# Weights rounded ahead of the mixed value in the late projection, and a new order of steps in the RWKV core

## The chip, the cores and the metric

The kernel runs on one core of a Trainium2 chip. The metric is the device time of one execution in microseconds; three executions of the kernel before gave 2173.88 us as median (2173.66 to 2179.12). TensorE is PE (its weight loads PEld), VectorE DVE, ScalarE ACT, GpSimd POOL, SyncE SP.

## The reference, cut to what matters

Two layers work on 256 tokens of width 2048 in fp32. What the change touches is the end of the first layer's second branch and, in the second layer, the recurrence of RWKV-7 together with the output projection of the attention half:

```
# first layer
yb = einsum('blc,cd->bld', yb * silu(zb), w_out_b)        # "outb"
m  = sigmoid(ga) * ya + sigmoid(gb) * yb                  # the mixed value
x  = x + einsum('bld,de->ble', m, w_o)                    # "wo"
# second layer, per head of 64, one token after the other
sa    = state @ a
state = state * w + sa (x) bb + v (x) k
y     = state @ r
# and then
mixed = concatenate([attn, rwkv]); h = h + mixed @ w_out  # attn half: "wouta", rwkv half: "woutb"
```

## The kernel before

Weights stream from HBM in units of 128 x 1024 fp32 through a ring of four slots. Each unit is made into two fp32r parts: ACT rounds it (`w_hi`, L506 in `split_hi`), DVE takes the rest (`w_lo`, L996 in `split_lo`), and SP reloads the slot as soon as `lo_ready` counts the unit. PE multiplies three times for each 128 x 128 block: high by high, high by low, low by high (L1714 to L1716). A unit of eight blocks is 24 matmuls with 256 columns. `split_hi` of unit n waits until unit n-4 has been used, `split_lo` until `split_hi` is done, and PE until `lo_ready`.

**Late projection (`outb`, 16 column blocks of one unit each).** For block b, ACT first rounds the weights of unit b+3, then waits for `f_ready` and rounds the mixed value f (L696, `ms`). DVE makes the low part of unit b+3, waits until PE has used unit b, computes f from the PSUM bank in two steps (L1250, L1252) and then the low part of the mixed value of block b-1 (L1243). `wo` follows; its first column reads the 16 mixed blocks one by one and waits for each.

**RWKV core.** The recurrence is done in four chunks of 64 tokens; each needs the inverse of a 64 x 64 triangular matrix per head, which a chain of products on PE gives. All 16 heads work at once: two heads share the 128 rows (row halves 0 and 1), and a step is 16 or 32 small matmuls, with an evacuation by DVE or ACT between steps. PE's order within chunk i is n2 and n2t (in one step), vt, n4 and n4t, w2, first half of x, w4 and n8, second half of x, bkt (transposes), w8, qt and q, q2 and md, g0, g1, g2, mt, n, sa, y, s. The sums w2, w4, w8 are added to `m_w` by DVE (L1538, `plus`). g0 and g2 (L1988, `with_a_and_r`) multiply the b and k of the next chunk by its a and r, the first for row half 0, the second for row half 1; DVE masks their results (L1442, L1443, `masked_products`; gm0 and gm1) into `g_a` and `g_r`. n (`a_with_b`) overwrites the PSUM banks of g0, and sa those of g2, so they wait for gm0 and gm1. Dependences are counted in `core_mm`, `core_dve` and `core_act`, by the tables MM, DV and AC.

Between these steps PE fills in blocks of `wouta` (`wout(count)`, L2040 to L2042, three matmuls each; 16 units of eight blocks). After step s of a chunk it does what is left of that chunk's share, PART = (4, 4, 3, 2, 3) units. The first block of unit j waits until DVE has added the result of unit j-2 to the residual (`wout_add`, L1519 and L1521, semaphore `wa_free`). DVE also splits the weights of these units (`wout_lo`) and weights the bonus (`gate_bonus`, L1480) within its own order. A stage ahead of chunk 0 (L1988 on `ps_main`) prepares that chunk's matrices.

Of the kernel before, what the change touches and what calls it, by code (L numbers as in the profile page):

```python
# [15 lines left out]
P = 128  # L16
# [110 lines left out]
def hybrid_kernel(nc, wmain, wdown, bst_dram, cst_dram, par_dram, const_dram, x_dram, lora_dram,  # L127
                  gup_dram, bias_dram, out_dram):
    ctx = ExitStack()
    with ctx:  # L130
# [195 lines left out]
        def bu_at(t):  # L326
# [4 lines left out]
        PIECES = ((0, 2), (2, 4), (4, 8), (8, 12), (12, 16))  # L331

        MM = {n: k + 1 for k, n in enumerate(
            ["n2", "n2t", "vt", "n4", "n4t", "w2", "w4", "n8", "x", "bkt", "w8", "qt", "q", "q2", "md", "g0", "g1",
             "g2", "mt", "n", "sa", "y", "s"])}
        DV = {n: k + 1 for k, n in enumerate(
            ["n2", "n4", "w2", "w4", "w8", "qt", "t1", "q2", "gm0", "g1", "gm1", "sa", "nf", "w1", "s"])}
        AC = {n: k + 1 for k, n in enumerate(["n2t", "vt", "n4t", "n8", "x", "bkt", "q", "md", "mt", "sa", "y"])}

        MM_NEXT, DV_NEXT = ("g0", "g2", "n", "s"), ("gm0", "gm1", "nf", "w1", "s")  # L340
# [159 lines left out]
        def _(act):  # L500
# [184 lines left out]
            for b in range(8):  # L685
                split_hi(At(n0 + b + 3))
                act.wait_ge(unit_used, n0 + b + 1)
                if b >= 2:
                    act.wait_ge(yo_ready, b - 1)
                nc.scalar.activation(gt[:, b % 2, :], main[:, (g0 + b) % 4, 0:L], ACT.Sigmoid,  # L690
                                     bias=par_c("b_glu", b)).then_inc(bank_free[(g0 + b) % 4], 1)
            n0 = UNIT0["outb"]
            for b in range(16):
                split_hi(At(n0 + b + 3))
                act.wait_ge(f_ready, b + 1)
                nc.scalar.activation(mh[:, b, :], f[:, b % 2, :], ACT.Copy).then_inc(mh_ready, 1)  # L696
            n0 = UNIT0["wo"]
            with act.Fori(0, 4) as i:
                for b in range(4):
# [286 lines left out]
        def _(dve):  # L986
# [12 lines left out]
            def bank(g):  # L999
                return main[:, g.c % 4, 0:L]  # L1000

            def evac(ins, g):

                return ins.then_inc(bank_free[g.c % 4], 1)
# [241 lines left out]
            for b in range(16):  # L1246
                split_lo(At(n0 + b + 3))
                dve.wait_ge(unit_used, n0 + b + 1)
                g = At(g0 + b)
                evac(V.tensor_tensor(tmp[:, 0, :], bank(g), sgb[:, b, :], ALU.mult), g)  # L1250
                dve.wait_ge(bank_free[g.c % 4], g.turns(4, 1))
                V.tensor_tensor(f[:, b % 2, :], tmp[:, 0, :], sga[:, b, :], ALU.add).then_inc(f_ready, 1)  # L1252
                if b:
                    mixed_lo(b - 1)
# [190 lines left out]
            def diagonal_t(h):  # L1445
                return V.tensor_tensor(mat["nt"][hrow(h), :, :], ga[hrow(h), h, :, :], mask("mdiagt", h), ALU.mult)
# [66 lines left out]
            def wout_lo():  # L1513
                split_lo(At(n0 + taken[0] + 3))
                taken[0] += 1
# [8 lines left out]
            def chunk(i, last=False):  # L1524
# [3 lines left out]
                def done(name, ins):  # L1528
                    ins.then_inc(core_dve, steps(DV, DV_NEXT, name, last))
                    dve.wait_ge(core_dve, i * len(DV) + DV[name])  # L1530

                def take(name, dst):
                    mm(name)
                    done(name, V.tensor_copy(flat(dst), heads(OUT[name])))

                def plus(name, dst, old):
                    mm(name)
                    done(name, V.tensor_tensor(flat(dst), flat(old), heads(OUT[name]), ALU.add))  # L1538

                take("n2", mat["n2"])  # L1540
                if i:
                    wout_add()
                    centre(i - 1, main[:, first_column(i) % 2, :])
                    take("n4", mat["n4"])
                else:
                    gate_bonus(0)
                    take("n4", mat["n4"])
                wout_lo()
                plus("w2", mat["w"], mat["w"])
                plus("w4", mat["w"], mat["w"])  # L1550
                if not last:
                    mm("bkt")
                    stage(i + 1)
# [5 lines left out]
                    gate_bonus(1)  # L1559
                take("q2", mat["n4"])  # L1560
                wout_lo()
                if not last:
                    mm("g0")
                    done("gm0", masked_products(0, G0, grs[(i + 1) % 2]))
                plus("g1", mat["n4t"], mat["n2t"])
                if not last:
                    diagonal_t(0)
                    mm("g2")
                    done("gm1", masked_products(1, G2, grs[(i + 1) % 2]))
                    diagonal_t(1)  # L1570
                    mm("n")
                    diagonal(OUT["n"])
                mm("sa")
                done("sa", V.tensor_copy(st[hrow(0), :, 0, :], by_head(OUT["sa"])[hrow(0), :, :]))
                if not last:
                    done("nf", rest(OUT["n"]))
                    done("w1", V.tensor_tensor(mat["w"][:, :, :], mat["nt"][:, :, :], eye, ALU.add))
                    if i:
                        gated(i - 1)
                        group_out(i - 1)  # L1580
                    mm("s")
                    link(V.tensor_tensor(state[:, :, :], state[:, :, :],
                                         S.rearrange("p (j n) -> p j n", n=CH), ALU.add))
                    done("s", V.tensor_tensor(state[:, :, :], state[:, :, :], pc[:, :, i:i + 1].to_broadcast([P, 8, CH]),
                                              ALU.mult))
                    for _ in range(PART[i] - 2):
                        wout_add()
                        wout_lo()
                else:
                    gated(i - 1)  # L1590
                    group_out(i - 1)
                    rwkv_low(1, slice(0, 2 * CH))
                    rwkv_low(2, tokens(2))
# [106 lines left out]
        def _(pe):  # L1700
# [281 lines left out]
                        ins = nc.tensor.matmul(head(banks, j, h), *fn(j, h), start=False, stop=(j % 4 == 3))  # L1982
                return ins

            def with_a_and_r(i, h, banks):

                for j in range(8):
                    ins = nc.tensor.matmul(banks[:, j // 4, (j % 4) * P:(j % 4 + 1) * P],  # L1988
                                           bkc[hrow(h), j, :, :].rearrange("p a n -> p (a n)"),
                                           abr[hrow(h), :, j, toks(i)], start=True, stop=True)  # L1990
                return ins

            def a_with_b(i, banks):
# [23 lines left out]
            pair_probs(PAIRS - 1)  # L2017
            pe.wait_ge(staged, 1)
            pe.wait_ge(gate_sb, 2)
            with_a_and_r(0, 0, main[:, 0:2, :]).then_inc(core_pre, 1)  # L2020
            with_a_and_r(0, 1, main[:, 2:4, :]).then_inc(core_pre, 1)
            pair_output(PAIRS - 1)
            a_with_b(0, A).then_inc(core_pre, 1)
            pe.wait_ge(gr_taken, 1)
# [22 lines left out]
            for i in range(NCH):  # L2047
# [81 lines left out]
                ac("q")  # L2129
                two(("q2", "nt", "n"), ("md", "w", None))  # L2130
                ac("bkt")
                if not last:
                    pe.wait_ge(staged, i + 2)
                    done("g0", with_a_and_r(i + 1, 0, G0))
                else:
                    wout(3)
                dv("t1")
                dv("q2")
                ac("md")
                prod("g1", "n4", "n2t")  # L2140
                if not last:
                    done("g2", with_a_and_r(i + 1, 1, G2))
                else:
                    wout(2)
                dv("g1")
                prod("mt", "md", "n4t")
                if not last:
                    dv("gm0")
                    done("n", a_with_b(i + 1, OUT["n"]))
                    dv("gm1")  # L2150
                else:
                    wout(2)
                ac("mt")
                done("sa", every_head(OUT["sa"], lambda j, h: (mat["n2"][hrow(h), j, :], xv[hrow(h), j, :])))
                wout(3 if not last else 1)
                dv("sa")
                ac("sa")
                by_halves(OUT["y"], lambda j, h: (state[hrow(h), j, :], br[hrow(h), j, toks(i)]))
# [227 lines left out]
```

## Time and profile before

| | us |
|---|---|
| median of three runs | 2173.88 |
| the profiled execution | 2174.53 |
| its span | 2172.9 |
| mean granted clock of TensorE | 0.998 |

The spans of all rows are of this one profiled execution; 1.6 us of its time lie outside its span. By engine, the busy shares of the span are PE 98%, PEld 96%, DVE 71%, ACT 48%, POOL 12%. A matmul's end is modelled and matmuls overlap, so a short stop of PE shows best as the distance between two starts. `outb` runs from 769 to 817 us, the stage ahead of chunk 0 from 1231.8 us, and the four chunks start at 1242.1, 1281.5, 1318.8 and 1353.8 us.

### The profile page before, as it was taken

The numbers are of one execution on the slowest core, as the hardware profiler recorded it, in microseconds if no ns is written. First come the engines' busy times: TensorE is split into PE (matmuls) and PEld (weight loads), VectorE is DVE, ScalarE is ACT, GpSimd is POOL, SyncE is SP. The second block draws the span as 40 slices with busy tenths as digits, with TensorE's granted clock in tenths as the row PEclk, the third lists the DMA queues.
The fourth block names the chain that finished last, engine by engine and source line by source line (L and its number), as shares of the span: only waits on it lengthen the run. The fifth ranks groups of instructions, "written<-read, shape, count | busy, mean of one in ns | idle before, by whom it ended". The sixth has DMA issues, their size and how long they took to land.

```text
span 2172.9 us, 51647 instructions
## 1 busy us (share of the span) xinstructions
PE 2127.8 (98%) x20608; PEld 2075.7 (96%) x20608; DVE 1543.2 (71%) x2015; ACT 1033.6 (48%) x1342; POOL 267.0 (12%) x178
## 2 busy tenths in 40 slices
PE   7999999999999999999999999999999999999997
PEld 7999999999999999999999889899999999999997
DVE  7889999999745677768867767776666666654554
ACT  6544444444454445556444454654444444444443
POOL 0354444445200000000001000000000000000000
PEclk9999999999999999999999999999999999999999
DMA  7555555555656556655655311355555655556654
GB/s 265 184 169 182 178 184 190 182 182 181 202 192 192 190 201 203 197 176 166 210 181 189 105 61 52 108 176 193 193 192 193 193 194 192 194 180 199 192 190 138
DMA packets 107106, 387.84 MB, mean 178 GB/s; under 512 B 12032, under 2 KB 12160, under 8 KB 106752
## 3 DMA queue, kind: packets, MB, share of 16 engines
q1 hardware_dynamic: 104400, 375.44, 52.9%
q0 software_dynamic: 2176, 9.78, 1.3%
q8 instruction: 74, 1.21, 0.2%
q10 hardware_dynamic: 432, 1.21, 0.1%
q14 instruction: 24, 0.20, 0.0%
HBM read 384.29 MB, written 2.10 MB: 178 GB/s over the span
## 4 chain that ended last, share of the span: by engine, by line
PE 79%; DVE 14%; issue 4%; ACT 2%; DMA 0%; DVEq 0%; SPq 0%; ACTq 0%
PE ps_main L1714 24%; PE ps_main L1715 23%; PE ps_main L1716 23%; DVE w_lo L996 6%; ACT w_hi L506 1%; DVE m L1155 1%; DVE m L1156 1%; PE ps_aux L2069 1%; DVE acc L1162 1%; PE ps_main L2040 1%; PE ps_main L2041 1%; PE ps_main L2042 1%; PE ps_main L1956 1%; DVE g_scan L1165 0%; DMA w_raw<-wmain 0%
## 5 line engine op out<-in xcount | busy, mean ns | idle before, releaser
L996 DVE TENSOR_TENSOR w_lo<-w_raw,w_hi 128x1024 fp32r<-128x1024 f32 x718 | 916.6, 1293 | 419.5 <-ACT w_hi L506 411.7
L506 ACT ACTIVATE w_hi<-w_raw 128x1024 fp32r<-128x1024 f32 x718 | 748.4, 1048 | 711.7 <-PE ps_main L1716 656.6
L1714 PE MATMUL ps_main<-xs,w_hi 128*128 128x256 f32 x1664 | 463.2, 278 | 7.6 <-DVE w_lo L996 6.6
L1715 PE MATMUL ps_main<-xs,w_hi 128*128 128x256 f32 x1664 | 460.2, 277 | 0.0
L1716 PE MATMUL ps_main<-xs,w_lo 128*128 128x256 f32 x1664 | 460.2, 277 | 0.0
L1714 PE MATMUL ps_main<-x3s,w_hi 128*128 128x256 f32 x1408 | 389.3, 276 | 0.0
L1715 PE MATMUL ps_main<-x3s,w_hi 128*128 128x256 f32 x1408 | 388.8, 276 | 0.0
L1716 PE MATMUL ps_main<-x3s,w_lo 128*128 128x256 f32 x1408 | 388.8, 276 | 0.0
L1714 PEld LDWEIGHTS ps_main<-xs,w_hi 128*128 128x128 f32 x1664 | 312.9, 188 | 16.0 <-DVE w_lo L996 11.6
L1716 PEld LDWEIGHTS ps_main<-xs,w_lo 128*128 128x128 f32 x1664 | 312.4, 188 | 0.0
L1715 PEld LDWEIGHTS ps_main<-xs,w_hi 128*128 128x128 f32 x1664 | 312.4, 188 | 0.0
L1714 PEld LDWEIGHTS ps_main<-x3s,w_hi 128*128 128x128 f32 x1408 | 264.3, 188 | 1.0 <-issue 1.0
L1715 PEld LDWEIGHTS ps_main<-x3s,w_hi 128*128 128x128 f32 x1408 | 264.3, 188 | 0.0
L1716 PEld LDWEIGHTS ps_main<-x3s,w_lo 128*128 128x128 f32 x1408 | 264.3, 188 | 0.0
L1714 PE MATMUL ps_main<-ns,w_hi 128*128 128x256 f32 x816 | 229.2, 281 | 0.1
L1716 PE MATMUL ps_main<-ns,w_lo 128*128 128x256 f32 x816 | 226.3, 277 | 0.0
L1715 PE MATMUL ps_main<-ns,w_hi 128*128 128x256 f32 x816 | 226.2, 277 | 0.0
L1714 PE MATMUL ps_main<-act,w_hi 128*128 128x256 f32 x704 | 194.3, 276 | 0.0
L1715 PE MATMUL ps_main<-act,w_hi 128*128 128x256 f32 x704 | 194.3, 276 | 0.0
L1716 PE MATMUL ps_main<-act,w_lo 128*128 128x256 f32 x704 | 194.3, 276 | 0.0
L1714 PEld LDWEIGHTS ps_main<-ns,w_hi 128*128 128x128 f32 x816 | 153.9, 189 | 7.4 <-issue 7.2
L1715 PEld LDWEIGHTS ps_main<-ns,w_hi 128*128 128x128 f32 x816 | 153.2, 188 | 0.2 <-issue 0.2
(428 smaller groups left out, 3724.4 us busy)
## 6 DMA issues: line engine op xcount, KB each, us to landing
w_raw<-wmain SPq DMA_DIRECT2D x622, 512.0 KB, 3.6
w_raw<-wdown SPq DMA_DIRECT2D x80, 512.0 KB, 3.7
w_raw<-wdown SPq DMA_DIRECT2D x16, 256.0 KB, 2.7
bias<-bias POOLq DMA_DIRECT2D x8, 384.0 KB, 3.4
x_res<-xt POOLq DMA_DIRECT2D x4, 512.0 KB, 7.0
out<-x_res SPq DMA_DIRECT2D x3, 512.0 KB, 2.8
x_first<-xt SPq DMA_DIRECT2D x2, 512.0 KB, 6.9
x_first<-xt ACTq DMA_DIRECT2D x2, 512.0 KB, 9.5
```

What stands on the lines that cost most here:

```text
L506: nc.scalar.activation(whi[:, s, 0:width], raw[:, s, 0:width], ACT.Copy).then_inc(hi_ready, 1)
L996: V.tensor_tensor(wlo[:, s, 0:width], raw[:, s, 0:width], whi[:, s, 0:width].bitcast(F32), ALU.subtract)\
L1155: V.tensor_tensor(m1[:, :, :], bu, cb, ALU.mult)
L1156: V.tensor_tensor(m2[:, :, :], bu, sb_, ALU.mult).then_inc(bu_used, 1)
L1162: link(V.tensor_tensor(g[:, 1, :], m1[:, 1, :], m2[:, 0, :], ALU.subtract))
L1714: nc.tensor.matmul(out, whi[:, s, w], high[:, k, :], start=(first and kk == 0), stop=False)
L1715: nc.tensor.matmul(out, whi[:, s, w], low[:, k, :], start=False, stop=False)
L1716: ins = nc.tensor.matmul(out, wlo[:, s, w], high[:, k, :], start=False, stop=(last and kk == kbs - 1))
L1956: ins = nc.tensor.matmul(head(banks, j, h), *fn(j, h), start=True, stop=True)
L2040: nc.tensor.matmul(out, whi[:, s, w], atth[:, k, :], start=(k == 0), stop=False)
L2041: nc.tensor.matmul(out, whi[:, s, w], attl[:, k, :], start=False, stop=False)
L2042: ins = nc.tensor.matmul(out, wlo[:, s, w], atth[:, k, :], start=False, stop=(k == 7))
```

## The change

Three things are changed.

First, in `outb`, ACT rounds the mixed value of block b-1 after the weights of unit b+3, not that of block b; DVE gets a wait on `f_ready` of the block before, ahead of writing `tmp` again.

Second, in the core's order on DVE: w2's sum comes right behind n4's copy, ahead of the weights' low part; in chunk 0 that low part and `gate_bonus(0)` move behind w4's sum. g1's sum moves ahead of gm0, and the two `diagonal_t` behind nf.

Third, in the core's order on PE: g0 and g2 become one step of 16 matmuls that alternates between the row halves, behind g1; four blocks of `wouta` take g0's old place, two more stand behind mt, and two in place of three behind sa.

```diff
+            def mixed_hi(j):
+                act.wait_ge(f_ready, j + 1)
+                nc.scalar.activation(mh[:, j, :], f[:, j % 2, :], ACT.Copy).then_inc(mh_ready, 1)
+
             for b in range(16):
                 split_hi(At(n0 + b + 3))
-                act.wait_ge(f_ready, b + 1)
-                nc.scalar.activation(mh[:, b, :], f[:, b % 2, :], ACT.Copy).then_inc(mh_ready, 1)
+                if b:
+                    mixed_hi(b - 1)
+            mixed_hi(15)
...
@@ DVE, outb
                 g = At(g0 + b)
+                if b:
+                    dve.wait_ge(f_ready, b)
                 evac(V.tensor_tensor(tmp[:, 0, :], bank(g), sgb[:, b, :], ALU.mult), g)
...
@@ DVE, chunk(i)
                 if i:
                     wout_add()
                     centre(i - 1, main[:, first_column(i) % 2, :])
-                    take("n4", mat["n4"])
-                else:
+                take("n4", mat["n4"])
+                plus("w2", mat["w"], mat["w"])
+                if i:
+                    wout_lo()
+                plus("w4", mat["w"], mat["w"])
+                if not i:
+                    wout_lo()
                     gate_bonus(0)
-                    take("n4", mat["n4"])
-                wout_lo()
-                plus("w2", mat["w"], mat["w"])
-                plus("w4", mat["w"], mat["w"])
...
                 wout_lo()
+                plus("g1", mat["n4t"], mat["n2t"])
                 if not last:
                     mm("g0")
                     done("gm0", masked_products(0, G0, grs[(i + 1) % 2]))
-                plus("g1", mat["n4t"], mat["n2t"])
-                if not last:
-                    diagonal_t(0)
                     mm("g2")
                     done("gm1", masked_products(1, G2, grs[(i + 1) % 2]))
-                    diagonal_t(1)
                     mm("n")
                     diagonal(OUT["n"])
...
                     done("nf", rest(OUT["n"]))
+                    diagonal_t(0)
+                    link(diagonal_t(1))
                     done("w1", V.tensor_tensor(mat["w"][:, :, :], mat["nt"][:, :, :], eye, ALU.add))
...
@@ PE
-            def with_a_and_r(i, h, banks):
-
+            def with_a_and_r(i, *banks):
+
+                ins = [None, None]
                 for j in range(8):
-                    ins = nc.tensor.matmul(banks[:, j // 4, (j % 4) * P:(j % 4 + 1) * P],
-                                           bkc[hrow(h), j, :, :].rearrange("p a n -> p (a n)"),
-                                           abr[hrow(h), :, j, toks(i)], start=True, stop=True)
+                    for h in range(2):
+                        ins[h] = nc.tensor.matmul(banks[h][:, j // 4, (j % 4) * P:(j % 4 + 1) * P],
+                                                  bkc[hrow(h), j, :, :].rearrange("p a n -> p (a n)"),
+                                                  abr[hrow(h), :, j, toks(i)], start=True, stop=True)
                 return ins
...
                 ac("bkt")
-                if not last:
-                    pe.wait_ge(staged, i + 2)
-                    done("g0", with_a_and_r(i + 1, 0, G0))
-                else:
-                    wout(3)
+                wout(4 if not last else 3)
                 dv("t1")
                 dv("q2")
                 ac("md")
                 prod("g1", "n4", "n2t")
                 if not last:
-                    done("g2", with_a_and_r(i + 1, 1, G2))
+                    pe.wait_ge(staged, i + 2)
+                    lower, upper = with_a_and_r(i + 1, G0, G2)
+                    done("g0", lower)
+                    done("g2", upper)
                 else:
                     wout(2)
                 dv("g1")
                 prod("mt", "md", "n4t")
                 if not last:
+                    wout(2)
                     dv("gm0")
...
-                wout(3 if not last else 1)
+                wout(2 if not last else 1)
```

**Order on ACT where `outb` begins.** `gt` is the last result of the projection before it, `ms` a mixed block. Before:

```order
L506 ACTIVATE w_hi<-w_raw 128x1024
L690 ACTIVATE gt<-ps_main,par 128x256
L506 ACTIVATE w_hi<-w_raw 128x1024
L696 ACTIVATE ms<-f_val 128x256
L506 ACTIVATE w_hi<-w_raw 128x1024
L696 ACTIVATE ms<-f_val 128x256
```

Now:

```order
L506 ACTIVATE w_hi<-w_raw 128x1024
L690 ACTIVATE gt<-ps_main,par 128x256
L506 ACTIVATE w_hi<-w_raw 128x1024 x2
L696 ACTIVATE ms<-f_val 128x256
L506 ACTIVATE w_hi<-w_raw 128x1024
L696 ACTIVATE ms<-f_val 128x256
```

The rows alternate as before, but each `ms` now belongs to the block before, so a weight unit no longer stands behind a mixed value that PE has yet to finish.

**Order on DVE where chunk 0 begins.** `m_n_139` and `m_n_141` are n2 and n4, `m_w` the sums, `sig_w` is `gate_bonus`, `bk_chunk` the staging of the next chunk. Before:

```order
L1534 COPY m_n_139<-ps_aux 128x512
L1480 SCALAR_TENSOR_TENSOR sig_w<-sig_w,par,out_gate_a 128x256 x4
L1534 COPY m_n_141<-ps_aux 128x512
L996 TENSOR_TENSOR w_lo<-w_raw,w_hi 128x1024
L1538 TENSOR_TENSOR m_w<-m_w,ps_aux 128x512 x2
L1366 COPY bk_chunk<-b_hat 64x8x64
```

Now:

```order
L1542 COPY m_n_139<-ps_aux 128x512
L1542 COPY m_n_141<-ps_aux 128x512
L1546 TENSOR_TENSOR m_w<-m_w,ps_aux 128x512 x2
L1002 TENSOR_TENSOR w_lo<-w_raw,w_hi 128x1024
L1488 SCALAR_TENSOR_TENSOR sig_w<-sig_w,par,out_gate_a 128x256 x4
L1374 COPY bk_chunk<-b_hat 64x8x64
```

The low part of the weights and the bonus have moved behind both sums, and stand ahead of the staging copies and of w8's sum.

**Order on PE in chunk 1, from the step behind q2 and md.** `ar_hat,bk_chunk` is the step with b and k, `m_n2t` g1, `m_n4t` mt, `bk_chunk,ar_hat` n, `x_chunk` sa, `att_h` a block of `wouta` (three rows each). Before:

```order
L2069 MATMUL ps_main<-const,m_w 64x64 x2
L1988 MATMUL ps_aux<-ar_hat,bk_chunk 128x128 x8
L1956 MATMUL ps_main<-m_n2t,m_n_141 64x64 x16
L1988 MATMUL ps_aux<-ar_hat,bk_chunk 128x128 x8
L1956 MATMUL ps_main<-m_n4t,m_md 64x64 x16
L1956 MATMUL ps_aux<-bk_chunk,ar_hat 64x64 x16
L1956 MATMUL ps_aux<-x_chunk,m_n_139 64x64 x16
```

Now:

```order
L2053 MATMUL ps_main<-att_h,w_lo 128x256
L1964 MATMUL ps_main<-m_n2t,m_n_141 64x64 x16
L1998 MATMUL ps_aux<-ar_hat,bk_chunk 128x128 x16
L1964 MATMUL ps_main<-m_n4t,m_md 64x64 x16
L2051 MATMUL ps_main<-att_h,w_hi 128x256
...
L1964 MATMUL ps_aux<-bk_chunk,ar_hat 64x64 x16
L1964 MATMUL ps_aux<-x_chunk,m_n_139 64x64 x16
```

The two steps of eight have become one of sixteen behind g1, with four blocks of the projection ahead of g1 and two between mt and n.

## Rows read from the trace of the kernel before

**Rows 1.** The page, busy time, share and instructions of each engine.

```profile
PE 2127.8 (98%) x20608; PEld 2075.7 (96%) x20608; DVE 1543.2 (71%) x2015; ACT 1033.6 (48%) x1342; POOL 267.0 (12%) x178
```

**Rows 2.** Waits of PE: waiting line, releaser, us in total, times, longest.

```profile
PE ps_aux L2069 <- DVE m_w L1538: 3.4, 3, 2.2
PE ps_main L1714 <- DVE ms L1243: 2.2, 1, 2.2
```

**Rows 3.** Timeline of ACT (start, us, line, tiles, idle before): end of glu, `outb`.

```profile
766.53 0.47 ACT L690 ACTIVATE gt<-ps_main,par 128x256 f32<-128x256 f32 x1 [1.30 <-PE ps_main L1716]
769.25 0.47 ACT L690 ACTIVATE gt<-ps_main,par 128x256 f32<-128x256 f32 x1 [1.30 <-PE ps_main L1716]
...
807.50 0.42 ACT L696 ACTIVATE ms<-f_val 128x256 fp32r<-128x256 f32 x1 [2.09 <-DVE f_val L1252]
807.83 1.04 ACT L506 ACTIVATE w_hi<-w_raw 128x1024 fp32r<-128x1024 f32 x1
810.96 0.42 ACT L696 ACTIVATE ms<-f_val 128x256 fp32r<-128x256 f32 x1 [2.09 <-DVE f_val L1252]
```

**Rows 4.** Timeline of DVE, one block of `outb`.

```profile
808.90 1.23 DVE L996 TENSOR_TENSOR w_lo<-w_raw,w_hi 128x1024 fp32r<-128x1024 f32 x1 [1.10 <-ACT w_hi L506]
810.04 0.42 DVE L1250 TENSOR_TENSOR tmp<-ps_main,sig_gb 128x256 f32<-128x256 f32 x1
810.50 0.43 DVE L1252 TENSOR_TENSOR f_val<-tmp,gate_a 128x256 f32<-128x256 f32 x1
```

**Rows 5.** Timeline of PE, first matmul of `outb`, and of `wo`'s k = 15.

```profile
769.04 0.28 PE L1714 MATMUL ps_main<-yos,w_hi 128*128 128x256 f32 x1
...
825.13 0.38 PE L1714 MATMUL ps_main<-ms,w_hi 128*128 128x256 f32 x1 [2.20 <-DVE ms L1243]
```

**Rows 6.** Timeline of PE, w4 and x of chunk 0, then of chunk 1.

```profile
1250.28 0.27 PE L2069 MATMUL ps_aux<-m_w,m_n 64*64 64x64 f32 x2 [2.17 <-DVE m_w L1538]
...
1251.49 1.92 PE L1975 MATMUL ps_aux<-stack,g_a 64*64 64x64 f32 x32
...
1288.48 0.27 PE L2069 MATMUL ps_aux<-m_w,m_n 64*64 64x64 f32 x2 [0.61 <-DVE m_w L1538]
...
1289.48 1.10 PE L1975 MATMUL ps_aux<-stack,g_a 64*64 64x64 f32 x32
```

**Rows 7.** Timeline of DVE, the two steps ahead of w2's sum in chunk 0.

```profile
1244.02 1.68 DVE L1480 SCALAR_TENSOR_TENSOR sig_w<-sig_w,par,out_gate_a 128x256 f32<-128x256 f32 x4
...
1248.32 1.23 DVE L996 TENSOR_TENSOR w_lo<-w_raw,w_hi 128x1024 fp32r<-128x1024 f32 x1 [1.75 <-ACT w_hi L506]
```

**Rows 8.** One stretch: busy time of each engine (instructions), granted clock, DMA share, GB/s.

```profile
1251.00:1254.40 3.40, 3.40 (x68) 3.28 (x60) 0.69 (x1) 1.78 (x3) 0.00 (x0) 0.50 0.35 130
```

**Rows 9.** Timeline of PE, the step with b and k: ahead of chunk 0, in chunk 1.

```profile
1231.80 3.47 PE L1988 MATMUL ps_main<-ar_hat,bk_chunk 64*128 64x128 f32 x32 [0.46 <-ACT out_gate_a L824]
...
1298.88 2.05 PE L1988 MATMUL ps_aux<-ar_hat,bk_chunk 64*128 64x128 f32 x16
1300.86 1.15 PE L1956 MATMUL ps_main<-m_n2t,m_n 64*64 64x64 f32 x32
1301.93 2.05 PE L1988 MATMUL ps_aux<-ar_hat,bk_chunk 64*128 64x128 f32 x16
```

**Rows 10.** Timeline of PE, a pair of row halves in the decay projection.

```profile
938.48 0.48 PE L1859 MATMUL ps_aux<-lora_lo,lora_up 64*128 64x256 f32 x1
938.48 0.48 PE L1860 MATMUL ps_aux<-lora_lo,lora_up 64*128 64x256 f32 x1
```

**Rows 11.** Timeline of PE and DVE: chunk 0's first sum; chunk 1, step s and behind.

```profile
1240.71 0.69 DVE L1474 TENSOR_TENSOR m_w<-m_nt,const 128x512 f32<-128x512 f32 x1
...
1310.41 1.10 PE L2164 MATMUL ps_aux<-stack,bk_tokens 128*64 128x64 f32 x32
1311.44 0.38 PE L2040 MATMUL ps_main<-att_h,w_hi 128*128 128x256 f32 x1
...
1313.54 0.42 DVE L1521 TENSOR_TENSOR x_res<-x_res,ps_main 128x256 f32<-128x256 f32 x1
```

More of the change, by code:

```diff
@@ L333, in hybrid_kernel @@
         MM = {n: k + 1 for k, n in enumerate(
-            ["n2", "n2t", "vt", "n4", "n4t", "w2", "w4", "n8", "x", "bkt", "w8", "qt", "q", "q2", "md", "g0", "g1",
+            ["n2", "n2t", "vt", "n4", "n4t", "w2", "w4", "n8", "x", "bkt", "w8", "qt", "q", "q2", "md", "g1", "g0",
              "g2", "mt", "n", "sa", "y", "s"])}
         DV = {n: k + 1 for k, n in enumerate(
-            ["n2", "n4", "w2", "w4", "w8", "qt", "t1", "q2", "gm0", "g1", "gm1", "sa", "nf", "w1", "s"])}
+            ["n2", "n4", "w2", "w4", "w8", "qt", "t1", "q2", "g1", "gm0", "gm1", "sa", "nf", "w1", "s"])}
         AC = {n: k + 1 for k, n in enumerate(["n2t", "vt", "n4t", "n8", "x", "bkt", "q", "md", "mt", "sa", "y"])}
@@ L2019, in _ @@
             pe.wait_ge(gate_sb, 2)
-            with_a_and_r(0, 0, main[:, 0:2, :]).then_inc(core_pre, 1)
-            with_a_and_r(0, 1, main[:, 2:4, :]).then_inc(core_pre, 1)
+            lower, upper = with_a_and_r(0, main[:, 0:2, :], main[:, 2:4, :])
+            lower.then_inc(core_pre, 1)
+            upper.then_inc(core_pre, 1)
             pair_output(PAIRS - 1)
```

## The prediction, made before the changed kernel had run

> **What bounds the kernel now.** I read the shares by engine first: PE is busy for 2127.8 us of a span of 2172.9 [rows 1], and DVE and ACT have room. So time can only come from work that PE no longer does, or from moments in which PE stands still. Then I read the waits of PE for whom it stands still: 3.4 us in three waits for `m_w`, and 2.2 us in one wait for `ms`, the low part of a mixed value [rows 2]. Both lie where the change is. The modelled ends hide part of such a stop, so I measure the stops by distances between starts.
>
> In `outb` the timeline of ACT shows the bound. In the projection before, one result follows the other after 2.72 us (766.53 to 769.25) [rows 3]: that is what PE needs for a unit of 24 matmuls, and ACT waits for PE. In `outb` it is 3.46 us (807.50 to 810.96), and ACT waits 2.09 us of each block for DVE's f [rows 3]. The cycle closes over two engines: `ms` starts at 807.50, the weights' high part at 807.83 for 1.04 us [rows 3], the low part at 808.90, tmp at 810.04, f at 810.50 for 0.43 us [rows 4], then the next `ms` at 810.96. PE is no member of it. The ring hides this for some blocks, then PE falls behind.
>
> **Part 1, the late projection.** PE begins `outb` at 769.04 and begins `wo`'s k-block 15 at 825.13, after the wait for `ms` [rows 5]. Between the two lie 16 units and 15 blocks of an eighth of a unit: 17.9 units. At 2.72 us they take 48.6 us, so a PE that never waits is there at 817.6. The difference is 7.5 us.
>
> Is PE unhindered after the change? ACT now rounds unit b+3 as soon as PE has used unit b-1, without waiting for f(b). High and low part take 1.04 + 1.23 = 2.3 us [rows 3, 4], and PE has three units (8.2 us) in hand. DVE does per block the low part (1.14, start to start), tmp and f (0.46 each) [rows 4] and the mixed low part (about as long as f, 0.4): 2.5 us in 2.72. ACT does 1.04 + 0.42. Both fit, DVE narrowly. The last mixed value: PE ends unit 15 at 769.04 + 43.5 = 812.6; tmp, f, high and low part come to 1.9 us, so 814.5, and PE asks for it at 817.6. The added wait on `f_ready` is for DVE's own previous step, and behind it stand only tmp and f; it costs nothing, since it is done one block earlier. **Term: -7.5 us**, between -7.0 (if DVE's narrow margin is missed by 0.03 us in each of 16 blocks) and -7.9.
>
> **Part 2, w2's sum.** In chunk 0, w4 starts at 1250.28 after 2.17 us of idle, for `m_w` [rows 6]. DVE has the bonus (1.68 us) and the weights' low part ahead of that sum, and the latter waits until 1248.32 for its high part [rows 7]. In chunk 1 the wait is 0.61 [rows 6]; all three together are 3.4 [rows 2], chunk 2's is about 0.2 since PE arrives late there. With the sum first, it is ready 0.9 us after w2 (0.04 to start, 0.69, 0.15 to PE), and the first half of x, 1.2 us, covers that. So all goes: -3.6. In chunk 0 the low part and the bonus (1.2 + 1.7) and the staging (1.5) now stand ahead of w8's sum, which comes 0.6 us too late for qt: +0.6. **Term: -3.0 us**, between -2.4 and -3.8.
>
> **Part 3, the clock.** Right behind the 2.17 us stop the granted clock is 0.50, the lower level of 1.2 GHz, for the 3.4 us from 1251.0, in which PE works throughout [rows 8]. The 16 products of x take 1.92 us there and 1.10 in chunk 1 [rows 6]. 3.4 us at half speed lose 1.7. The stop goes, so I count **-1.7 us**, between 0 and -1.7. The new stops below are 1.5 us or less; I give a fall 1 in 4.
>
> **Part 4, b and k in one step.** 16 matmuls ahead of chunk 0 take 3.47 us, 217 ns each, one after the other; in a chunk each eight take 1.98 us (1298.88 to 1300.86, and 1301.93 to the next step) [rows 9]. They use 64 rows each. Does the other half run beside it? The decay projection says so: two matmuls on opposite row halves, each with all 128 columns, start at the same 938.48 [rows 10]. So I take 16 in the time of eight, 1.98 us, three times: **-5.9 us**. Bounds: nothing gained (0) if the alternating loads of different weights keep them apart, since [rows 10] show only one pair at a time; the full -5.9 on the other side. I take the full value, because the rows are the same shape but for 128 columns of data in place of 256.
>
> Ahead of chunk 0 PE would gain another 1.7 us, but DVE is next: its masks start when the first half's result is there, which stays as it was, and its chain ends with the sum at 1240.71 + 0.69 [rows 11], less 0.15 us of idle between its masks. PE could start at 1241.3, and started chunk 0 at 1242.1: **-0.8 us**.
>
> **Part 5, the projection's blocks as filler.** Their number is fixed; only their places change. There are two stretches more in each of three chunks. The first matmul of a stretch is modelled at 0.38 us against 0.28 of one within [rows 5, 11], and leaving costs as much: 0.2 us a stretch, 6 stretches, **+1.2 us**, between 0.6 and 2. The Trainium skill has a rule here, in "TensorEngine Tiling (Array Packing)", section Key Properties: a change of the tiling mode drains the engine. If each of these 12 changes laid open what a matmul outlasts its successor's start by (0.28 less 0.11, so 0.17 us), this would be +2.0, and the sum 0.8 us later. By this rule the sum moves within its range.
>
> **Part 6, what is late next.** DVE. Taking chunk 1 in times of before, with g0's old start at 1298.88: four blocks (1.6 us), then g1 at 1300.5, b and k at 1301.6 to 1303.6, mt, two blocks (0.9), n at 1305.4, sa at 1306.4 (behind gm1, which DVE ends at 1306.2 after 2.6 us of masks), two blocks, y at 1308.4, s at 1310.6 to 1311.6. Sixteen blocks are left there, two units, and the second begins at 1314.4. It needs the add of the unit two before. On DVE stand ahead of it: masks until 1306.2, n's diagonal, sa's copy until 1308.2, nf 0.7, both diagonals 1.4, w1 0.7, the gate and output of the chunk before 2.3, the state 1.5, the add 1.0: 1315.8, where before it ended at 1313.96 [rows 11] and PE had 21 blocks left. PE waits 1.5 us. The same in chunk 0, without the gate and output but with 0.7 us less filler ahead: 0.6 us. g1 in chunk 0 waits 0.4 longer for q2's copy, which stands behind `gate_bonus(1)`; y waits 0.1 in each chunk; chunk 3 starts with a DVE that is 0.3 late for n4. **Term: +3.0 us**, between 1 and 5.
>
> **The sum.** -7.5 -3.0 -1.7 -5.9 -0.8 +1.2 +3.0 = -14.7 us. The profiled execution took 2174.5 (2172.9 of span and 1.6 around it), which gives 2159.8. The median of the runs is 0.65 us below it, so 2159.2 us. Behind the core nothing changes: chunk 3 and the 24 blocks behind it have the same order and end in the same wait.
>
> **The rivals.**
> - *The pair doesn't overlap.* 16 matmuls take 3.5 to 4.0 us. Part 4 gives nothing, and gm0 comes later. For it: each of the 16 has weights of its own; in [rows 9] PE goes at 217 ns per matmul with no overlap at all. Against it: [rows 10]. Price: 5.9 lost in the chunks and 1.1 ahead of chunk 0, where the first half's result comes 1.7 late: 2166.2 us. Chance 0.10.
> - *The half clock stays.* PE now has more short stops in chunk 0 (0.8, 0.5, 0.6, 0.7 us) and one of 1.5 behind chunk 1. Each fall as before costs 1.7. One remains: 2160.9; two: 2162.6. Chance 0.20.
> - *DVE is later still in the chunks' ends.* The adds wait for units, the units for adds: if every chunk's end cost 2 us rather than 1.5, 0.6 and 0, this would be +3.9: 2163.1. Chance 0.08.
> - *Slower than before.* The place is the core, 1231 to 1391 us; the mechanism the clock again, not as one dip but as a state: half-speed PE in front of late sums. With 30 us at 1.2 GHz the 14.7 us are gone, and beyond this it is slower; 45 us would give 2181.7. Against it: in the trace 3.4 us is all that the worst stop caused, and the stretches of projection are dense. Chance 0.02.
>
> **How the numbers follow.** Forecast 2159.2, chance 0.60 together with the small deviations of its terms. The rivals take 0.40. The low end, all terms at their good ends (-7.9, -3.8, -5.9, -0.8, -1.7, +0.6, +1), would be -18.5; I go two thirds of the way from -14.7, to 2156. The high end takes in one or two dips of the clock and the late DVE, and stops short of the pair that doesn't overlap: 2165. Outside lie 0.10 to 0.15 above and a little below. What a measurement of this kernel can tell from no change is about 0.3%, 6.5 us. The forecast, the clock's dips, the late DVE and even the pair that doesn't overlap (2166.2, 0.35% below) are faster; within 0.3% falls that last rival with a dip on top, and an `outb` that wins only half: 0.04. Slower: 0.02.
>
> **What would show it.** In `outb`, `ms` after `ms` at 2.72 us from the first block on, no wait of PE for `ms`, and `wo` reached 7.5 us earlier; a distance of over 2.8 would say that DVE is the bound. In the chunks, 16 matmuls of b and k within 2 us; no wait of w4 for `m_w`; no stretch at clock 0.50 behind 1240 us; new waits of the projection's first matmul (unit 3, unit 7) for `x_res` of L1521's successor, 0.6 and 1.5 us. The core's first step to `woutb` would shrink by 7.2 us. I am wrong if that sum is under 3 or if the distance in `outb` stays above 3 us.

## The result and the profile after

| | before | changed | ratio (95% interval) |
|---|---|---|---|
| first comparison, median us | 2174.31 | 2157.44 | 0.9913 (0.9897 to 0.9930) |
| profiled execution, us | 2174.53 | 2159.07 | |
| its span, us | 2172.9 | 2157.4 | |

The changed kernel is faster: by its ratio 18.9 us of the 2173.88 shown, by the two profiles 15.5. The forecast was -14.7, and 2159.2 us between 2156 and 2165; the ratio makes 2155.0. The shares by engine, against [rows 1]: PE's busy time is 9.8 us less (the paired steps and the half clock that is gone), the rest of the 15.5 is idle time.

```profile
PE 2118.0 (98%) x20608; PEld 2067.1 (96%) x20608; DVE 1544.4 (72%) x2015; ACT 1033.1 (48%) x1342; POOL 268.6 (12%) x178
```

I cut both traces at PE's first matmul of each stage and of each chunk; a distance between two such starts holds every stop and slow matmul in it.

| distance between starts, us | before | changed | difference | forecast |
|---|---|---|---|---|
| `outb` to `lora` (outb and wo) | 138.71 | 130.56 | -8.15 | -7.5 |
| `lora` to the first step with b and k | 324.05 | 324.38 | +0.33 | 0 |
| that step to chunk 0 | 10.30 | 9.48 | -0.82 | -0.8 |
| chunk 0 | 39.41 | 35.73 | -3.68 | -3.8 |
| chunk 1 | 37.29 | 36.74 | -0.55 | -0.6 |
| chunk 2 | 35.04 | 33.01 | -2.03 | -1.7 |
| chunk 3 to `woutb` | 38.80 | 37.89 | -0.91 | -0.3 |

All else, ahead and behind, is within 0.3 us.

**The late projection.** ACT's timeline in `outb`, after; it answers to [rows 3].

```profile
785.76 1.06 ACT L506 ACTIVATE w_hi<-w_raw 128x1024 fp32r<-128x1024 f32 x1 [1.17 <-PE ps_main L1724]
786.72 0.40 ACT L696 ACTIVATE ms<-f_val 128x256 fp32r<-128x256 f32 x1
788.48 1.06 ACT L506 ACTIVATE w_hi<-w_raw 128x1024 fp32r<-128x1024 f32 x1 [1.35 <-PE ps_main L1724]
789.44 0.40 ACT L696 ACTIVATE ms<-f_val 128x256 fp32r<-128x256 f32 x1
```

The distance between two `ms` is 2.72 us, where it was 3.46, and ACT now waits for PE (in two blocks of this profile for the weights' DMA), and for f only in the last block. DVE keeps up in the same 2.72 (tmp at 780.26 and 782.98):

```profile
780.26 0.43 DVE L1258 TENSOR_TENSOR tmp<-ps_main,sig_gb 128x256 f32<-128x256 f32 x1 [0.34 <-PE ps_main L1724]
780.72 0.43 DVE L1260 TENSOR_TENSOR f_val<-tmp,gate_a 128x256 f32<-128x256 f32 x1
781.06 0.42 DVE L1249 TENSOR_TENSOR ms<-f_val,ms 128x256 fp32r<-128x256 f32 x1
781.75 1.23 DVE L1002 TENSOR_TENSOR w_lo<-w_raw,w_hi 128x1024 fp32r<-128x1024 f32 x1 [0.27 <-ACT w_hi L506]
782.98 0.43 DVE L1258 TENSOR_TENSOR tmp<-ps_main,sig_gb 128x256 f32<-128x256 f32 x1
```

And PE never stops. The first line below is the window from 770 to 826 us: its length, then busy us and instructions of PE, PEld, DVE, ACT and POOL, then granted clock, DMA share and GB/s. PE is busy throughout. The second line, from PE's timeline, is `wo`'s first matmul. It starts 16 times 2.72 us behind `outb`'s at 769.18.

```profile
770.00:826.00 56.00, 56.00 (x497) 56.00 (x496) 47.45 (x81) 27.50 (x41) 2.68 (x5) 1.00 0.68 237
```

```profile
812.70 0.28 PE L1722 MATMUL ps_main<-ms,w_hi 128*128 128x256 f32 x1
```

**The core.** PE's timeline, the step with b and k ahead of chunk 0 and in chunks 0 and 1; it answers to [rows 9] (each of the 16 matmuls has two records).

```profile
1224.12 2.06 PE L1998 MATMUL ps_main<-ar_hat,bk_chunk 64*128 64x128 f32 x32 [0.46 <-ACT out_gate_a L830]
...
1253.44 2.06 PE L1998 MATMUL ps_aux<-ar_hat,bk_chunk 64*128 64x128 f32 x32
...
1288.73 2.06 PE L1998 MATMUL ps_aux<-ar_hat,bk_chunk 64*128 64x128 f32 x32
```

The next steps begin at 1226.10, 1255.43 and 1290.72: both row halves take 1.98 us. x's second half in chunk 0 takes 1.10 us in place of 1.92 [rows 6], and the window that was at clock 0.50 in [rows 8] is at 1.00; what takes the old stops' place is in the last block below, from the table of PE's waits between 1222 and 1395 us (first line: the projection's units 3 and 7; second: g1, for q2's copy; third: qt, for w8's sum).

```profile
1240.41 1.10 PE L1983 MATMUL ps_aux<-stack,g_a 64*64 64x64 f32 x32
```

```profile
1251.00:1254.40 3.40, 2.85 (x56) 2.62 (x56) 3.18 (x5) 3.24 (x8) 0.00 (x0) 1.00 0.00 0
```

```profile
PE ps_main L2051 <- DVE x_res L1529: 1.5, 2, 1.2
PE ps_main L1964 <- DVE m_n L1542: 0.5, 1, 0.5
...
PE ps_aux L2080 <- DVE m_w L1546: 0.5, 1, 0.5
```

### The profile page after: what moved, and what is told of

Same layout as the page of the kernel before. It is cut to its first block, busy times and chain, and to the rows that moved or that the text cites. A ratio compares the mean times of both kernels' runs of the same rounds, so it can differ in the third digit from the quotient of the medians.

```text
span 2157.4 us, 51664 instructions
## 1 busy us (share of the span) xinstructions
PE 2118.0 (98%) x20608; PEld 2067.1 (96%) x20608; DVE 1544.4 (72%) x2015; ACT 1033.1 (48%) x1342; POOL 268.6 (12%) x178
## 4 chain that ended last, share of the span: by engine, by line
PE 82%; DVE 12%; issue 3%; ACT 1%; DMA 1%; DVEq 0%; SPq 0%; ACTq 0%
PE ps_main L1722 25%; PE ps_main L1724 24%; PE ps_main L1723 24%; DVE w_lo L1002 5%; DVE m L1161 1%; DVE m L1162 1%; PE ps_aux L2080 1%; DVE acc L1168 1%; PE ps_main L2051 1%; PE ps_aux L1964 1%; DMA w_raw<-wmain 1%; ACT w_hi L506 0%; DVE g_scan L1171 0%; PE ps_main L1964 0%; PE ps_main L2052 0%
```

## The experiments

The ratio is to the kernel before on the same chip. Stage distances are those of the table above, from each run's own profile.

**The changed kernel again, and a third time.**

> The changed kernel a third time, beside the version with VectorE's idle stretches filled. Theory: the profiles' sum of -15.5 us is the true size, so 0.9929 of before (between 0.992 and 0.9937), and the first 0.9913 was scatter of four executions. Rival: the first comparison was right, 0.9913 or less, and the profiles miss 3 us. The stage of woutb goes at 118 ns per matmul, as in both profiles of this program, if that pitch belongs to the program; at 113 if it is chance.

The first repetition is the same kernel:

> The changed kernel once more, in five rounds against the one before. By the trace of its profiled execution the late projection gives 8.2 us and the core 7.9, less 0.6 us that lie elsewhere: 15.5 us, ratio 0.9929. Theory 'the steps are all there is': the ratio of paired runs comes out at 0.9920 to 0.9935, and runs of 2155 us belong to chips or moments in which the kernel before is quicker too. Rival 'a second gain that only some executions show': runs fall into two groups 3.7 us apart (2155.5 and 2159.3) while the kernel before stays in one, and the ratio is 0.9913 or less.

Measured: 2158.72 us, 0.9927 (0.9913 to 0.9941), and 2156.77 us, 0.9923 (0.9909 to 0.9936). The stage with `outb` took 130.56 both times, the core 154.87 and 153.27 (152.85 in the first profile). The three ratios stand for -18.9, -15.9 and -16.7 us; their intervals overlap, and none tells more than "about 17". The profiles' 15.5 (ratio 0.9929) lies in all three intervals, in the first's just inside its upper end. The theory of the first repetition held, and its rival fell: the executions don't form two groups (2156.9 to 2162.3 us, and the kernel before beside them went from 2172.2 to 2180.3). `woutb`'s pitch doesn't belong to the program, it changes between executions (last section).

**The late projection alone.** Only these lines of the change:

```
+                if b:
+                    mixed_hi(b - 1)
+            mixed_hi(15)
...
+                if b:
+                    dve.wait_ge(f_ready, b)
```

> Only the order of the late projection is changed (weights rounded ahead of the mixed value), the core is as before. Theory: PE is never stopped in outb, 7.5 to 8.3 us less, ratio 0.9962 to 0.9966. Rival 'the gain is given back in wo or the norm behind it': under 5 us, ratio over 0.9977. Rival 'this part is worth more than the trace showed in some executions': over 10 us, ratio under 0.9954.

Measured: 2164.07 us, 0.9956 (0.9942 to 0.9970), so -9.6 us; the expected 0.9962 to 0.9966 lies inside the interval. The stage takes 130.55. So all of the stage's -8.2 is this edit's. For what the ratio has beyond that the profile has candidates that are no doing of the edit, none of them tested: with the old order and the old 2.2 us stop, chunk 0 had no stretch at half clock this time (37.92 us in place of 39.41), and `woutb` went at its faster pace (last section).

**The core alone.** The rest of the change, with the late projection as before.

> Only the core is changed, the late projection is as before. Theory: 7.2 to 8 us less, ratio 0.9963 to 0.9967, and with the run of the projection alone it adds up to the whole. Rival 'the second gain sits in the core': over 10 us, ratio under 0.9954. Rival 'the clock still falls': a stretch at 0.50 behind the stage ahead of chunk 0 and 1.7 us less gain.

Measured: 2168.66 us, 0.9973 (0.9964 to 0.9982), -5.9 us, less than the 7.2 to 8 expected. Its core took 153.12, like the changed kernel's, 7.7 less than before. But here `outb` to `lora` took 140.26 in place of 138.71: behind the stop for `ms` (2.3 us) lay a stretch at half clock, which the rival had expected ahead of chunk 0. -7.7 and +1.55 are -6.2. The two parts' ratios add up to -15.5 us; the whole change, measured beside them, made -15.9.

**The rows one after the other.** Both row halves in one step, but not alternating:

```
-                for j in range(8):
-                    for h in range(2):
+                for h in range(2):
+                    for j in range(8):
```

> The changed kernel, but the 16 matmuls with b and k go through row half 0 first and then row half 1, in the same place. Theory 'opposite row halves run side by side': four steps take 3.5 us in place of 2.0, so three in the chunks cost 1.7 to 2 us each, DVE's masks start 1.7 us later in each, and the time is 6 to 8 us above the changed kernel (ratio to before 0.996 to 0.9975). Rival 'the halves don't overlap, the step is short for another reason': within 1 us of the changed kernel.

Measured: 2163.70 us, 0.9948 (0.9935 to 0.9962); 5.0 us above the changed kernel measured beside it, which has the same instructions. Expected were 6 to 8, and a ratio of 0.996 to 0.9975: both missed, by little. The lead to chunk 0 is back at its old 10.30 us. PE's timeline in chunk 1; the next step starts at 1295.41:

```profile
1291.99 3.50 PE L1998 MATMUL ps_aux<-ar_hat,bk_chunk 64*128 64x128 f32 x32
```

3.42 us against 1.99: alternating the halves is what lets them overlap, though each matmul loads weights of its own. Of the 1.98 us that a chunk gained, 1.43 are the pair's; the other 0.55 came from having one step in place of two.

**w2's and w4's sums first, alone.**

```
+                take("n4", mat["n4"])
+                plus("w2", mat["w"], mat["w"])
+                if i:
+                    wout_lo()
+                plus("w4", mat["w"], mat["w"])
+                if not i:
+                    wout_lo()
+                    gate_bonus(0)
```

> The kernel before with one edit: in the core VectorE adds w2 and w4 ahead of the weights' low part (and, in chunk 0, of the bonus). Theory: three waits of TensorE for m_w (3.4 us by the table) go, w8's sum comes 0.6 us late in chunk 0: -3.0 us, so 0.9986 of before, and the core's first step to woutb takes 156.0 us where no 0.50 clock stretch falls into it (the late-projection experiment, with the old order, took 159.0 without one). Rival 1: the 2.2 us stop is what makes the clock fall; then before always has that stretch, and this edit is worth -4.7 us (0.9978). Rival 2: the waits come back behind the sums (for qt, g1, the projection): under 1 us.

Measured: 2171.87 us, 0.9981 (0.9972 to 0.9990), -4.1 us. The core took 156.09, as expected; PE's waits for m_w there fell from 3.4 us in three [rows 2] to w8's alone (0.5). Against a core with the old order and no half clock (158.99) that is -2.9, against the profile of before -4.75. The ratio's interval holds both the theory's 0.9986 and the first rival's 0.9978, so it doesn't decide between them. The late-projection run does: the stop doesn't always bring the half clock, so that rival falls.

**Without the two added stretches of projection blocks.**

```
-                wout(4 if not last else 3)
+                if last:
+                    wout(3)
...
-                    wout(2)
...
-                wout(2 if not last else 1)
+                wout(3 if not last else 1)
```

> The changed kernel with the projection's blocks where they stood before: none ahead of g1, none behind mt, three behind sa; in chunks 0 to 2. Theory: TensorE then waits in each of them for VectorE's copy of q2 and ScalarE's of md (about 1.4 us ahead of g1), and for the masks (0.4 ahead of n, 0.4 ahead of sa); two stretches of filler less give 0.4 back, and the wait of unit 7 (1.2 us) goes: +3 to +5 us against the changed kernel. Rival: the filler only pays its entrances, and the waits are hidden: -1 us.

Measured: 2161.87 us, 0.9941 (0.9927 to 0.9954). Against the three ratios of the changed kernel this is 3 to 6 us more. The core took 159.10 us, 3.0 more than with w2's and w4's sums first alone (156.09), of which at most 1.7 are a half-clock stretch: without the blocks the paired step doesn't pay. PE's timeline, chunk 0's g1, then chunk 1's g1, n and sa:

```profile
1253.20 1.32 PE L1964 MATMUL ps_main<-m_n2t,m_n 64*64 64x64 f32 x32 [2.29 <-DVE m_n L1542]
...
1291.24 1.15 PE L1964 MATMUL ps_main<-m_n2t,m_n 64*64 64x64 f32 x32 [1.43 <-ACT m_md L879]
...
1295.81 1.15 PE L1964 MATMUL ps_aux<-bk_chunk,ar_hat 64*64 64x64 f32 x32 [0.36 <-DVE g_r_even L1451]
1297.14 1.03 PE L1964 MATMUL ps_aux<-x_chunk,m_n 64*64 64x64 f32 x28 [0.18 <-DVE g_r_even L1451]
```

The waits are where the theory had them, 1.43 ahead of g1; the one ahead of sa is 0.2 smaller. I had missed chunk 0, where DVE still has the second bonus ahead of q2's copy: 2.29 us, and right behind that stop the window at half clock, which this stop cost on top (the paired step took 3.40 us there):

```profile
1254.00:1257.40 3.40, 3.40 (x41) 3.28 (x38) 0.90 (x2) 1.68 (x5) 0.00 (x0) 0.50 0.44 154
```

**DVE's idle stretches filled.** From the changed kernel:

```
                 if not i:
-                    gate_bonus(1)
+                    gate_bonus(0)
...
                 plus("g1", mat["n4t"], mat["n2t"])
+                if not i:
+                    gate_bonus(1)
+                elif not last:
+                    gated(i - 1)
...
-                        gated(i - 1)
-                        group_out(i - 1)
...
                     for _ in range(PART[i] - 2):
                         wout_add()
                         wout_lo()
+                    if i:
+                        group_out(i - 1)
```

(and `gate_bonus(0)` gone from its place ahead of w8, ACT's `gate_weight` behind sa's copy)

> The changed kernel, VectorE's work that nobody waits for moved into its idle stretches: in chunk 0 the first bonus stands behind t1 and the second behind g1's sum (ScalarE scales the gate behind sa's copy), in chunks 1 and 2 the gate stands behind g1's sum and the group's output behind the last add. Theory: the waits for w8's sum (0.5) and for g1 (0.55) in chunk 0 go, and unit 7's wait for x_res in chunk 1 (1.2) goes; unit 3's grows from 0.3 to 0.6: -2.0 us against the changed kernel. Rival: VectorE is the bound of the chunks' ends, the moved work comes due there or delays the next chunk's n2: between -0.5 and +1.

> The version with the bonus, the gate and the group's output in VectorE's idle stretches, again. Theory: 2.0 us less in the core than the changed kernel (150.8 where no stretch at clock 0.50 falls into it), and 1.7 us less in woutb if the pitch of 113 ns belongs to the program: together 3 to 4 us below the changed kernel of the same batch. Rival: only the core's 2.0.

Measured: 2156.42 us, 0.9913 (0.9898 to 0.9928), and 2155.14 us, 0.9910 (0.9897 to 0.9924); beside it the changed kernel had 0.9923. The two differ by 1.6 us in the medians of that batch, and intervals of ratio overlap, so the times alone don't show it. The profiles do: chunk 0 takes 35.25 and 35.21 us (35.73, 36.02 and 35.72 in the changed kernel's three), chunk 1 35.13 and 35.28 (36.74, 36.48, 36.51). Together that is 70.4 and 70.5 against 72.5, 72.5 and 72.2: the 2 us that were expected. Over the whole core the second profile has 151.51 (150.8 expected; 152.85, 154.87 and 153.27 in the changed kernel's); the rest is scatter in chunks 2 and 3. The wait of qt for w8's sum in chunk 0 is gone, and the table of waits has 0.4 for the add, where it was 1.5; DVE's timeline, second profile, shows the add of chunk 1 at 1300.21, 1.97 us behind the state's first step, where the gate and output no longer stand ahead of the latter:

```profile
1298.24 0.69 DVE L1590 TENSOR_TENSOR state<-state,ps_aux 128x512 f32<-128x512 f32 x1 [0.69 <-PE ps_aux L2177]
1298.97 0.69 DVE L1592 TENSOR_TENSOR state<-state,chunk_decay 128x512 f32<-128x512 f32 x1
1299.69 0.48 DVE L1527 SCALAR_TENSOR_TENSOR x_res<-x_res,par,rstd 128x256 f32<-128x256 f32 x1
1300.21 0.42 DVE L1529 TENSOR_TENSOR x_res<-x_res,ps_main 128x256 f32<-128x256 f32 x1
```

The wait for q2's copy ahead of g1 in chunk 0 stayed (0.5): DVE is late there whichever bonus stands ahead.

**The kernel before, one more profile.**

> The kernel before once more, for its profile. Theory: stretches at granted clock 0.50 (3.4 us, 1.7 us lost each) fall by chance behind stops of TensorE, in the late projection or in the core's chunk 0; without one the stage outb to lora takes 138.8 us and the core 159.0. Rival: chunk 0's stop always brings it, and the core takes 160.8 again.

Measured: 2177.68 us. 138.73 for `outb` to `lora`, 161.01 for the core: the half clock in chunk 0 again, 39.39 us. That is the rival's number. But its "always" is excluded by the late-projection run; with it, chunk 0 of the old order had the half clock in two of three profiles.

## Why the mechanisms held, and which step of the prediction failed

**What held.** Each mechanism came with its sign and in its place: `ms` every 2.72 us and `wo` reached by a PE that never waits; 16 matmuls of b and k in 1.98 us; w2's sum gone from the waits; no half clock in the core (in none of the changed kernel's three profiles); the waits of units 3 and 7, 0.34 and 1.18 us, where 0.6 and 1.5 stood; g1's 0.55 and w8's 0.52. The lead to chunk 0 and chunks 0 and 1 came out within 0.12 us, in the first profile. The rival that the pair doesn't overlap is excluded: the serial run shows what it would have cost.

**What failed is the range's low end.** The ratio of the first comparison makes 2155.0 us of the 2173.88, one us under my 2156. Much of this is chance: 2155.0 lies under all four executions of the changed kernel in that comparison (2155.3 to 2159.6), the ratio of the two medians is 0.9922, and both repetitions' ratios (2158.0 and 2157.1 us) lie inside the range. The step of the prediction that failed is how the range was made: it put at nothing what executions of one program differ by. And part 1, its largest term, was mis-sized.

The mis-sized terms:

- *Part 1, -7.5; measured -8.15.* The stage takes 130.56 us in all eight profiles with the new order, against 138.7. I let 15 blocks pass between `wo`'s start and the wait. It is 14: the same matmul starts at 817.46 in the changed kernel, 4.76 us behind 812.70, and a block is 0.34. The other 0.34 is a cost that I hadn't counted: behind the wait PE didn't go on at once at its pace. Its timeline in the kernel before, the matmuls behind the one at 825.13 [rows 5]:

```profile
825.35 0.28 PE L1715 MATMUL ps_main<-ms,w_hi 128*128 128x256 f32 x1
825.47 0.28 PE L1716 MATMUL ps_main<-ms,w_lo 128*128 128x256 f32 x1
825.70 0.38 PE L1714 MATMUL ps_main<-ms,w_hi 128*128 128x256 f32 x1
825.92 0.28 PE L1715 MATMUL ps_main<-ms,w_hi 128*128 128x256 f32 x1
```

  Three of these distances (825.13, 825.47 and 825.70 to the next) are 0.22 us where 0.11 is the pace. A second profile of the kernel before has the same three.
- *Parts 2 and 6, in chunks 2 and 3: forecast -2.0, measured -2.9, -1.0 and -2.3 in the changed kernel's three profiles.* What moves between the three is PE's "issue" stops (last section); without those, on both sides, the three are -2.5, -2.3 and -2.6. I had put the third wait of m_w in the table [rows 2] at the right price; it stood in chunk 3. But w4's 64 matmuls behind it took 1.30 us, 1.00 in the changed kernel: the second matmul started 0.3 us behind the first. That is so in all three profiles of the old order, but not in chunk 1, where the same step behind the same wait of 0.61 us took 1.00 [rows 6]; why is open. Nor did the 0.3 for n4 in chunk 3 come. Against this, the 0.2 that I counted for chunk 2 stands in no row: that profile has no such wait there.

```profile
1360.82 0.59 PE L2069 MATMUL ps_aux<-m_w,m_n 64*64 64x64 f32 x3 [0.61 <-DVE m_w L1538]
```

The range: executions of the changed kernel went from 2155.3 to 2162.3 us in three comparisons. I took the profile of before, which had one half-clock stretch in the core, as typical of all; the profiles since then show such stretches in other places or not at all, and three more differences of that size (below). A forecast by one profile can't be surer than those: plus or minus 3 us at least. Even with all terms at their good ends my sum made 2155.4 us, more than the 2155.0 of the ratio, and by my rule of two thirds of the way the low end would have been 2156.7, not 2156. The ratio has 3.4 us more than the two profiles; which of these differences the other executions of the first comparison had is not known, since one of each was profiled.

**Part 3** was right for the pair of profiles (chunk 0: -3.68, forecast -3.8), with some luck: the profile before happened to have the stretch. It cost 1.5 us there, not 1.7 (39.41 with it, 37.92 without). So this is not a certain gain: the price of a stop of over 2 us is 1.5 us times a chance. The core as a whole (forecast -7.2; -8.0, -6.0 and -7.6 by the three profiles against the first of before) scatters more than its forecast was off.

**Part 5.** A stretch of four blocks ahead of g1 runs from 1286.08 to 1287.66, PE's timeline of the changed kernel:

```profile
1286.08 0.38 PE L2051 MATMUL ps_main<-att_h,w_hi 128*128 128x256 f32 x1
1286.30 0.29 PE L2052 MATMUL ps_main<-att_l,w_hi 128*128 128x256 f32 x1
...
1287.45 0.28 PE L2053 MATMUL ps_main<-att_h,w_lo 128*128 128x256 f32 x1
1287.66 0.33 PE L1964 MATMUL ps_main<-m_n2t,m_n 64*64 64x64 f32 x4
```

12 matmuls in 1.58 us are 0.22 more than 12 times 0.1133 (a unit's 2.72 over 24), so 0.2 for entering and leaving was right, here at least. The Trainium skill, "TensorEngine Tiling (Array Packing)", section Key Properties, has a change of tiling mode drain the engine. The trace agrees that each change costs (0.22 and 0.21 us at the two ends in place of 0.11), but the 0.33 for two changes that I had worked out for it, an estimate, was too much.

## What to carry to other kernels

When two engines take turns in a cycle that the busiest engine isn't part of, break it. Let one of them do the next block's work ahead of its turn. When matmuls use half of the rows each, alternate the halves, and put other work between them and whoever waits for their sums: without those blocks 3 to 6 us of the gain went into new waits. Price a stop by the distance to the first matmul that runs at full pace again, not by the wait in the table.

## What the runs showed of the hardware

- *The half clock is a chance, not a rule.* In the twelve profiles PE stopped nine times for over 2 us once it had begun. The core's stop (2.2 us, old order) was followed by 3.4 us at 0.50 in two of three; the one of 2.29 us in the run without the blocks was, too; the one for `ms` in `wo` (2.2 to 2.3) in two of four; one of 2.02 us at 127 us was not. So five of nine. Shorter stops brought it as well. At the start of the program, near 17 us, it came behind all three stops of 1.84 to 1.87 us, and behind none of those of 0.9 to 1.5. At 127 us it came behind one stop of 1.77; the other profiles have 1.0 to 2.0 us there without it. The window is from the changed kernel's second profile:

```profile
17.60:21.00 3.40, 3.40 (x17) 3.40 (x18) 3.40 (x6) 3.40 (x5) 0.00 (x0) 0.50 0.13 53
```

  And once it came without a stop ahead: in the first profile with the idle stretches filled, 6.8 us from 1220.7, with no wait of PE in the table for the 25 us ahead, in the sparse work ahead of chunk 0 (the b and k step took 3.56 us in place of 1.98):

```profile
1220.70:1227.50 6.80, 6.80 (x40) 5.17 (x42) 0.00 (x0) 1.96 (x4) 0.00 (x0) 0.50 0.00 0
```

- *The same stage has two paces.* `woutb` takes 45.33 us in five of twelve profiles and 43.65 in seven, with nothing in the stage but the mean of its matmuls to tell them apart. It is not the program: the changed kernel shows both, here its first and its third profile (groups of PE by line and shape between 1380 and 1415 us; busy us, mean ns):

```profile
L1723 PE MATMUL ps_main<-rwkv_l,w_hi 128*128 128x256 f32 x100 | 28.1, 281 | 0.0
```

```profile
L1723 PE MATMUL ps_main<-rwkv_l,w_hi 128*128 128x256 f32 x104 | 28.7, 276 | 0.0
```

  The distance between two starts is 0.118 or 0.1135 us. The granted clock is 1.00 in both. What sets it is open.
- *PE sometimes stops where no other engine holds it up* ("issue"), for 0.2 to 0.8 us, mostly in the core's chunks 2 and 3 and at other steps each time: 0.3 us in all in the changed kernel's first profile, 2.0 in the second, 0.9 in the third. The DMA queue of the kind "instruction" gives the likely cause. Between 1200 and 1400 us the twelve profiles have 23 such stops of over 0.1 us, and behind every one PE goes on 2.2 to 2.7 us after a transfer of that queue began (in the second profile transfers begin at 1310.0, 1313.9 and 1346.3 us, and PE goes on at 1312.24, 1316.23 and 1348.75). These transfers begin some 5 us apart, and most bring no stop. So PE probably waited for its own instructions; no run tested it.
- The start of `outb` itself, ahead of which nothing was changed, moved between 768.45 and 771.70 us.
